# A fused two-model forward pass in fp32: the RMS norms and head norms through one column per token half

## The reference

```python
# first stack, two layers; rmsnorm(x, g) = x * rsqrt(mean(x*x, -1) + eps) * g
x = x + even_mixer(rmsnorm(x, norm_mix[0]), ...)              # gated MLP + forgetting attention
x = x + memory_cross_attention(rmsnorm(x, ...), rmsnorm(mem, ...), ...)
x = x + swiglu(rmsnorm(x, norm_ffn[0]), ...)
x = x + odd_mixer(rmsnorm(x, norm_mix[1]), ...)               # differential attention + short conv
x = x + memory_cross_attention(...)
x = x + moe_swiglu(rmsnorm(x, norm_ffn[1]), ...)              # 8 experts, top 2
x = rmsnorm(x, norm_final)
# second stack, two layers l, modulated by c
h = rms_norm(x, norm1_w[l]) * (1 + sc1) + sh1
x = x + g1 * hybrid_mixer(h, ...)                             # retention + HGRN2
h = rms_norm(x, norm2_w[l]) * (1 + sc2) + sh2
x = x + g2 * conv_ffn(h, ...)
return rms_norm(x, final_norm_w)

def head_norm(o, w):                                          # per head of 128 channels
    return o * rsqrt(mean(o * o, -1) + eps) * w               # then times a silu gate in the second stack
```

## Time and profile before

| | |
|---|---|
| device time, median of 3 runs | 2598.55 us (2595.91 to 2599.55) |
| profiled execution | 2602.0 us, its span 2600.2 us |
| PE busy | 2425.7 us (93%) in 14784 matmul records |
| DVE busy | 1975.0 us (76%) in 2569 |
| ACT busy | 1539.6 us (59%) in 2088 |

### The profile page before, as it was taken

One profiled execution on the slowest core, in us unless ns is written; L12 is line 12 of the kernel. 1 busy time (PEld: TensorE's weight loads), 2 busy tenths in 40 slices (PEclk: granted clock), 3 DMA queues, 4 the chain that ended last, 5 costly groups with the idle time before them and its releaser, 6 DMA issues.

```text
span 2600.2 us, 39070 instructions
## 1 busy us (share of the span) xinstructions
PE 2425.7 (93%) x14784; PEld 2064.8 (79%) x14784; DVE 1975.0 (76%) x2569; ACT 1539.6 (59%) x2088; POOL 4.4 (0%) x8
## 2 busy tenths in 40 slices
PE   7998999989899999999999999997968999976998
PEld 6997998989767676767676767666858998866998
DVE  5755787976488888888888888885766886767664
ACT  4654444445377777777777777775344554543553
POOL 0000000000000000000000000000000000000000
PEclk9999999999899999999999999998988998998999
DMA  8344689544469898989898989891312666421440
GB/s 347 136 156 162 230 305 356 203 162 180 177 259 351 334 352 328 351 328 350 329 350 329 350 328 350 331 386 64 132 65 98 259 236 234 183 76 65 172 170 17
DMA packets 87980, 623.65 MB, mean 240 GB/s; under 512 B 9732, under 2 KB 11304, under 8 KB 12968
## 3 DMA queue, kind: packets, MB, share of 16 engines
q1 hardware_dynamic: 87312, 621.28, 62.9%
q10 hardware_dynamic: 536, 0.53, 0.1%
HBM read 620.72 MB, written 1.05 MB: 239 GB/s over the span
## 4 chain that ended last, share of the span: by engine, by line
PE 89%; DVE 8%; ACT 2%; issue 1%; DMA 0%; ACTq 0%; DVEq 0%; SPq 0%
PE bank L625 13%; PE bank L623 13%; PE bank L624 13%; PE bank L647 11%; PE bank L643 11%; PE bank L644 11%; PE bank L745 2%; PE bank L742 2%; PE bank L744 2%; PE bank L691 2%; PE bank L998 2%; DVE Z L1826 1%; PE bank L935 1%; DVE ring_r L1495 1%; PE bank L946 1%
## 5 line engine op out<-in xcount | busy, mean ns | idle before, releaser
L1495 DVE TENSOR_TENSOR ring_r<-ring,ring_r 128x1024 fp32r<-128x1024 f32 x402 | 490.8, 1224 | 284.5 <-ACT ring_r L1113 284.2
L643 PE MATMUL bank<-XH,ring_r 128*128 128x256 f32 x2208 | 565.7, 292 | 75.4 <-ACT XH L1149 32.1
L1113 ACT ACTIVATE ring_r<-ring 128x1024 fp32r<-128x1024 f32 x402 | 423.5, 1056 | 347.0 <-PE bank L647 176.2
L644 PE MATMUL bank<-XH,ring_r 128*128 128x256 f32 x2208 | 559.9, 289 | 0.0
L643 PEld LDWEIGHTS bank<-XH,ring_r 128*128 128x128 f32 x2208 | 438.7, 199 | 85.5 <-issue 37.0
L1900 DVE TENSOR_TENSOR ring_r<-ring,Z_r 128x1024 fp32r<-128x1024 f32 x336 | 411.1, 1225 | 50.6 <-ACT Z_r L1374 50.6
L644 PEld LDWEIGHTS bank<-XH,ring_r 128*128 128x128 f32 x2208 | 439.1, 199 | 0.1
L1900 DVE TENSOR_TENSOR ring_r<-ring,mhat_r 128x1024 fp32r<-128x1024 f32 x336 | 408.0, 1220 | 36.7 <-ACT mhat_r L1374 35.0
L1374 ACT ACTIVATE mhat_r<-ring 128x1024 fp32r<-128x1024 f32 x336 | 356.3, 1063 | 108.6 <-PE bank L625 106.9
L1374 ACT ACTIVATE Z_r<-ring 128x1024 fp32r<-128x1024 f32 x336 | 356.5, 1062 | 103.8 <-PE bank L625 103.8
L624 PE MATMUL bank<-ring_r,xn_r 128*96 128x512 f32 x896 | 352.2, 393 | 0.0
(11 more groups left out here) (297 smaller groups left out, 3424.9 us busy)
## 6 DMA issues: line engine op xcount, KB each, us to landing
ring<-in_experts SPq DMA_DIRECT2D x336, 1024.0 KB, 6.8
ring<-in_stream SPq DMA_DIRECT2D x246, 1024.0 KB, 7.0
ring<-in_stream SPq DMA_DIRECT2D x6, 512.0 KB, 5.3
xT<-in_xT SPq DMA_DIRECT2D x2, 512.0 KB, 5.3
mhat<-in_memT SPq DMA_DIRECT2D x1, 1024.0 KB, 16.7
swap<-in_early SPq DMA_DIRECT2D x1, 1024.0 KB, 18.6
swap<-in_late SPq DMA_DIRECT2D x1, 1024.0 KB, 9.8
out_T<-xn SPq DMA_DIRECT2D x8, 128.0 KB, 2.0
```

The costliest lines, as they stand in the source:

```text
L643: pe.matmul(dst, hi[:, a], x_hi(kb), start=(n == 0), stop=False)
L644: pe.matmul(dst, lo[:, a], x_hi(kb), start=False, stop=False)
L1113: act.activation(wh(Q), raw(Q), ACT.Copy).then_inc(sems["whi"], 1)
L1495: dve.tensor_tensor(raw(Q, ring_r), raw(Q), wh(Q).bitcast(F32), ALU.subtract).then_inc(sems["wlo"], 1)
```

## The change

The norms' factor is computed once per token on a column instead of on all partitions.

Norms: DVE adds the squares of blocks 1 to 6 (in norms 4, 10 and 12: 1 to 5) onto block 0, each add linked to the one before by a semaphore (`add_squares`). PE then multiplies block 0 and the one (two) left over, as weights, by one column of ones: per block two matmuls, one per half of 128 tokens; the result is 128x2, token on partition. Root and reciprocal run on 128x2 (`rcol`). Two matmuls with the column broadcast as weights and the identity as moving operand spread it over the partitions (`norm_spread`); the apply step reads the factor from PSUM. In norms 1, 2 and 5 the spread comes later in PE's order. ACT's squares of norms 3, 9 and 11 are put between weight quarters.

Head norms: ACT squares each head straight out of PSUM, PE makes eight one-column matmuls, root and reciprocal run on 128x8 (`hcol`), eight matmuls spread them into two banks. Meanwhile DVE multiplies the products, out of PSUM, by gain and gate (`head_scaled`), and by the factor at the end (`head_normed`). In `b{l}` the first spread follows the second group's products on PE.

```diff
-            def norm(i):
-                key = f"nrm{i}"
-                G.wait_free(pe, key)
-                for kb in range(KB):
-                    W(pe, "sq", i, kb + 1)
-                    mm = pe.matmul(bank[G.bank(key)][:, 0:S], ones, sqb(i, kb), start=(kb == 0), stop=(kb == KB - 1))
-                G.filled(mm, key)
+            def norm_sums(i):              # direct(i) is 2 for i in (4, 10, 12), else 1
+                key, first = f"nrm{i}", KB - direct(i)
+                G.wait_free(pe, key)
+                W(pe, "sqa", i)
+                for n, kb in enumerate([0] + list(range(first, KB))):
+                    if n:
+                        W(pe, "sq", i, kb + 1)
+                    for t in range(NT):
+                        mm = pe.matmul(bank[G.bank(key)][:, t:t + 1], sqb(i, kb)[:, t * P:(t + 1) * P], ones[:, 0:1],
+                                       start=(n == 0 and t == 0), stop=(kb == KB - 1), skip_group_check=True)
+                G.filled(mm, key)
+            def norm_spread(i):
+                key = f"spread{i}"
+                G.wait_free(pe, key)
+                W(pe, "rc", i)
+                for t in range(NT):
+                    mm = pe.matmul(bank[G.bank(key)][:, t * P:(t + 1) * P], rcol[:, i % 2, t:t + 1].to_broadcast([P, P]),
+                                   ident, start=True, stop=True)
+                G.filled(mm, key)
+            def head_norm_sums(i, sq):
+                key = f"hn{i}"
+                G.wait_free(pe, key)
+                for h in range(H):
+                    W(pe, "hsq", i, h + 1)
+                    for t in range(NT):
+                        n = 2 * h + t
+                        mm = pe.matmul(bank[G.bank(key)][:, n:n + 1], sq[:, n * P:(n + 1) * P], ones[:, 0:1],
+                                       start=True, stop=True)
+                G.filled(mm, key)
+            def head_norm_spread(i):
+                W(pe, "hrc", i)
+                for g in range(2):
+                    key = f"hb{i}"
+                    G.wait_free(pe, key, g)
+                    for n in range(4):
+                        mm = pe.matmul(bank[G.bank(key, g)][:, n * P:(n + 1) * P],
+                                       hcol[:, 4 * g + n:4 * g + n + 1].to_broadcast([P, P]), ident, start=True, stop=True)
+                    G.filled(mm, key, g)
...
                 linear_pv(f"b{l}.rpv", rv, mhf)
-                head_norm(1 + 2 * l, zs(8))
+                head_norm_sums(1 + 2 * l, zs(8))
...
                 linear_pv(f"b{l}.hpv", hi, zs(0, 2))
-                head_norm(2 + 2 * l, zs(5))
+                head_norm_spread(1 + 2 * l)
+                head_norm_sums(2 + 2 * l, zs(5))
+                head_norm_spread(2 + 2 * l)
...
-            def head_norm(i, pvkey, Y, sq):
+            def head_norm(i, pvkey, sq):
+                for h in range(H):
+                    G.wait_full(act, pvkey, h)
+                    act.activation(sq[:, h * S:(h + 1) * S], bank[G.bank(pvkey, h)][:, 0:S], ACT.Square)\
+                        .then_inc(sems["hsq"], 1)
+                key = f"hn{i}"
+                G.wait_full(act, key)
+                G.drained(act.activation(hcol, bank[G.bank(key)][:, 0:8], ACT.Sqrt, scale=1.0 / P, bias=eps), key)
...
-            def norm(i, src=xT, dst=xn):
+            def add_squares(i, kbs):
+                for kb in kbs:
+                    W(dve, "sq", i, kb + 1)
+                    ins = dve.tensor_tensor(sqb(i, 0), sqb(i, 0), sqb(i, kb), ALU.add)
+                    if kb == KB - direct(i) - 1:
+                        ins.then_inc(sems["sqa"], 1)
+                    else:
+                        dlink(ins)
+            def norm_column(i):
                 G.wait_drained(dve, f"nrm{i}")
-                dlink(dve.reciprocal(rstd[:, :], rms[:, i % 2, :]))
+                dve.reciprocal(rcol[:, i % 2, :], rcol[:, i % 2, :]).then_inc(sems["rc"], 1)
+            def norm_apply(i, src=xT, dst=xn):
+                key = f"spread{i}"
+                G.wait_full(dve, key)
                 g = gcol(i)
                 for kb in range(KB):
-                    dve.scalar_tensor_tensor(out=dst[:, kb, :], in0=src[:, kb, :], scalar=g(kb), in1=rstd[:, :],
-                                             op0=ALU.mult, op1=ALU.mult).then_inc(sems["xn"], 1)
+                    dve.scalar_tensor_tensor(out=dst[:, kb, :], in0=src[:, kb, :], scalar=g(kb),
+                                             in1=bank[G.bank(key)][:, 0:S], op0=ALU.mult, op1=ALU.mult)\
+                        .then_inc(sems["xn"], 1)
+                W(dve, "xn", i, KB)
+                G.drained(dve.memset(tiny[:, 255:256], 0.0), key)
...
             G.drained(dve.tensor_copy(line[:, :], bank[G.bank("line")][0:H, 0:SPAN]), "line")
-            norm(1, mhat, mhat)
+            add_squares(1, range(1, 7))
+            norm_column(1)
...
                     G.drained(ins, key, g)      # residual of ffn{i}, g in 0..3
+                    if g:
+                        add_squares(4 if i == 0 else 8 + 2 * i, ((), (1,), (2, 3), (4, 5))[g])
...
                     residual(f"b{l}.res", o + 16, [m])
                     low()
+                    if m == 4:
+                        add_squares(9 + 2 * l, range(1, 4))
+                    elif m in (5, 6):
+                        add_squares(9 + 2 * l, [m - 1] if m == 5 else [5, 6])
...
-                head_norm(1 + 2 * l, zs(9), zs(8), lambda h: col("ret_w", 4 * l + h), zs(7))
+                head_scaled(1 + 2 * l, f"b{l}.rpv", zs(9), lambda h: col("ret_w", 4 * l + h), zs(7))
+                head_column(1 + 2 * l)
+                for h in range(H):
+                    G.wait_drained(dve, f"b{l}.hg", h)
+                head_scaled(2 + 2 * l, f"b{l}.hpv", zs(10), lambda h: col("hgrn_w", 4 * l + h), zs(3))
+                for h in range(H):
+                    G.wait_drained(dve, f"b{l}.rpv", h)
+                head_normed(1 + 2 * l, zs(9))
+                head_column(2 + 2 * l)
                 rows_low(f"b{l}.out", zs(9), 0)
-                head_norm(2 + 2 * l, zs(10), zs(5), lambda h: col("hgrn_w", 4 * l + h), zs(3))
+                for h in range(H):
+                    G.wait_drained(dve, f"b{l}.hpv", h)
+                head_normed(2 + 2 * l, zs(10))
```

More of the change, by code:

```diff
@@ L393, in build @@
         G.plan("nrm0", 1)
-        for k, n in (("f.q", 4), ("f.f", 1), ("f.k", 4), ("line", 1), ("nrm1", 1), ("f.S", 4), ("f.v", 2), ("f.u", 4),
+        G.plan("spread0", 1)
+        for k, n in (("f.q", 4), ("f.f", 1), ("f.k", 4), ("line", 1), ("nrm1", 1), ("f.S", 4), ("spread1", 1), ("f.v", 2), ("f.u", 4),
                      ("f.vv", 2), ("f.pT", 4), ("f.gm", 4), ("f.pv", 4), ("f.res", 8)):
@@ L398, in plan_mem @@
         def plan_mem(l, i):
-            for k, n in ((f"m{l}.k", 4), (f"nrm{i}", 1), (f"m{l}.k4", 4), (f"m{l}.q", 8), (f"m{l}.S", 4), (f"m{l}.v", 4),
+            for k, n in ((f"m{l}.k", 4), (f"nrm{i}", 1), (f"m{l}.k4", 4), (f"spread{i}", 1),
+                         (f"m{l}.q", 8), (f"m{l}.S", 4), (f"m{l}.v", 4),
                          (f"m{l}.pT", 4), (f"m{l}.pv", 4), (f"m{l}.res", 8)):
@@ L406, in plan_ffn @@
             G.plan(f"nrm{ni}", 1)
+            G.plan(f"spread{ni}", 1)
             for j in range(FB // 2):
@@ L657, in split_ready, with proj_f @@
                         lambda kb: W(pe, "xl", 0, low_base[inst] + order.index(kb) + 1))
-            def proj_f(nm, j, key, x_hi=xh, x_lo=xl, have=(ready, ready), order=range(KB)):
+            def proj_f(nm, j, key, x_hi=xh, x_lo=xl, have=(ready, ready), order=range(KB), between=None):
                 for m in range(4):
+                    if m == 1 and between:
+                        between()
                     i = 4 * j + m
@@ L821, in mem_attention @@
                        (lambda kb: W(pe, "mh", l, kb + 1), lambda kb: W(pe, "ml", l, kb + 1)))
-                norm(ni)
-                proj_f(f"m{l}.k", 1, f"m{l}.k", mh, ml)
+                norm_sums(ni)
+                proj_f(f"m{l}.k", 1, f"m{l}.k", mh, ml, between=lambda: norm_spread(ni))
                 for j in range(2):
@@ L1123, in root @@
                 G.wait_full(act, key)
-                G.drained(act.activation(rms[:, i % 2, :], bank[G.bank(key)][:, 0:S], ACT.Sqrt, scale=1.0 / D, bias=eps),
+                G.drained(act.activation(rcol[:, i % 2, :], bank[G.bank(key)][:, 0:NT], ACT.Sqrt, scale=1.0 / D, bias=eps),
                           key)
@@ L1268, in ffn @@
                 squares(ni, kbs=range(0, 4))
-                prep(3)
-                squares(ni, kbs=range(4, 8))
+                for kb in range(4, 7):
+                    prep()
+                    squares(ni, kbs=[kb])
+                squares(ni, kbs=[7])
                 root(ni)
@@ L1580, in _ @@
             dve.wait_ge(const_in, 32)
+            add_squares(0, range(1, 7))
             norm(0)
@@ L1678, in mem_attention @@
                 vm = zs(4, 2)
-                low(4)
```

(14 more changed lines are left out.)

101 lines of the change are left out of this document (57 added, 44 removed).

## The result

The kernel after takes 2558.19 us (median of 4 runs, 2555.78 to 2559.76) where the kernel before takes 2598.88 (4 runs beside it, 2595.91 to 2599.55): ratio 0.985, 95% interval 0.984 to 0.986, a gain of 40.7 us. The forecast was 2546, its range 2531 to 2563. The direction, the place and the range were right; the gain is 11.6 us less than the 52.3 forecast. The profiled execution took 2559.0 us (span 2557.2), 0.8 above the median, while that of before, at 2602.0, was 3.1 above the 2598.9 measured here. So the two profiles differ by 43.0 us and the medians by 40.7: 2.3 us of the 11.6 are the distance between these executions and their medians, and 9.3 us are terms of the sum (52.3 against 43.0).

The account below looks back on a forecast made before the run. TensorE, with 89% of the chain of waits, plus its holes was taken to bound the kernel. Norms 14.3, late head norms 34 and o layer 4 sum to 52.3 us; 2602.0 less that, less 3.45, gives 2546 us, range 2531 to 2563.

Parts of the forecast that it names:

- What bounds the kernel, and the reciprocals: Whole kernel: TensorE holds 89% of the chain of waits; reciprocals of 6.55 and 1.75 us fall to near 0.2 us.
- Prices: New instructions: one-column matmul 0.22 us at full clock, 0.44 at half; linked add 0.46; apply step 0.48, no more than before.
- C (dear): All 164 new matmuls: broadcast-column weights or one-column matmuls are dear; at 0.82 us each 2644 us; chance 0.04.
- E (free): The 98 one-column sums cost next to nothing, giving back 11 us: 2535 us; chance 0.04.
- Late head norms: Head norms of the two late layers: wait before the output projection goes, 17 us gained a layer, 34 for both.
- Rival A: Late layers pay half clock all through, 8 us a layer: 2562 us; chance 0.14.
- The o layer: Head norm of the o layer: the waiting projection products start at 551.4 instead of 554.42, 4 us gained.
- Norm 1: Norm 1: adds come late, TensorE waits 4.8 us, scores of f.S start at 58.4 instead of 56.35; 2.45 us lost.
- Norms 3 and 4: Norms 3 and 4: linked adds on VectorE delay residuals and sums; 1.2 us lost in norm 3, 1.9 in norm 4.
- Norms 7, 8 and 10: Gains from shorter sums and tails: 2.4 us in norm 7, 0 in norm 8, 2.0 in norm 10.
- The norms as a whole: All thirteen norms: gains and losses of the column form together give 14.3 us gained.
- Rival B: Holes get short enough that the clock holds behind the norms too, 15 us more gained: 2531 us; chance 0.13.

Follow-up runs that it names:

- eighth run: Kernel after with each one-column sum matmul of the two late layers' head norms done twice, 32 records in a row instead of 16: 2568.56 us, ratio 0.990.
- third run: Kernel after with norm 1's six adds moved earlier, three and three behind the first two k-head copies: 2548.03 us, ratio 0.982.
- sixth run: Kernel after with norm 3 summed without adds by sixteen one-column matmuls, norm 4's six adds behind its last residual: 2551.27 us, ratio 0.983.
- seventh kernel: Kernel after with norm 1's adds earlier, norm 3 without adds, norm 4's adds behind its last residual: 2543.55 us, ratio 0.9795; run again 2546.22 us, 0.981.
- fifth run: Kernel after with norm 1 without adds, its sixteen one-column matmuls in two rows behind the first two heads' scores: 2551.48 us, ratio 0.9825.
- second run: Kernel after with the head norms as before, so only the thirteen norms go through columns: 2591.35 us, ratio 0.998.
- fourth run: Kernel after with norm 1 without adds, all eight blocks summed by sixteen one-column matmuls in one row: 2553.91 us, ratio 0.984.
- first run: Kernel before with only the head norms through columns, the thirteen norms as before: 2555.63 us, ratio 0.9845.

## Why the prediction came out as it did

- **What bounds the kernel, and the reciprocals**: right. Reciprocals take 0.17 and 0.20 us.
- **Prices**: right. One-column record at full clock 0.105 us (0.11 said), at half 0.23 (1.84 / 8), four spread records 0.44 where their column is ready. The eight apply steps with an operand in PSUM take 3.22 us, as the old ones did (3.25). Rivals C (dear) and E (free) are out: the eighth run's 32 records took 3.47 us. The Trainium skill's page TensorE: Matmul & The Clock Gate (Back-to-back issue gap) has a floor of 25 ns for a matmul of so few columns, by which, as an estimate, they would take 0.8 us. The same section gives that floor for an isolated gap and says that in a stream of weight load and matmul pairs both set the spacing; the 0.108 us a record here, each with its own weights, agrees with that and not with the floor alone. The prediction set its rows against the floor alone.
- **Late head norms**: right, 17.2 and 17.0 against 17 each, with a hole of 0.59 us where I said 0.7. The 1.5 us missing in the first profile are a clock dip of one execution. Rival A (half clock all through) did not come true, but the eighth run shows that its mechanism is real: rows twice as long bring the half clock.
- **The o layer**: 4.8 and 4.65 against 4. Right.
- **Norm 1, the step that failed most**: "the scores of f.S start at 58.4 ... 2.45 lost". The hole was as said (4.89 us against 4.8). The scores started at 56.47, with norm 0's 2.95 us gained ahead, so 1.0 us later than said. What I left out is that the hole costs the clock: sums at 1.84 instead of 0.87, the scores 10.0 us instead of 6.9. I had priced half clock behind the holes of the other norms, but took this one for a plain wait. The third run removes the hole and gets 8.7 us back.
- **Norms 3 and 4**: the mechanism (linked adds ahead of a residual on DVE) is shown by the sixth run; 0.75 and 0.4 us more than forecast were lost. The sums of norm 4 started 3.8 us later than before's place in the stream, as said.
- **Router and first expert**: the forecast had nothing there. Sixteen L1043 records take 5.41 us where the profile before, the third run and others have 3.91, with PE in the same order of work. The two profiles of the kernel after, the two of the seventh kernel and that of the fifth all lose 2.5 to 2.6 us there; the second, third, fourth and sixth kernel, with the same norm 6, lose nothing. Two stand between: the first, with the old norm 6, loses 1.0 us at the router and nothing in the first expert, and the eighth loses 1.9 us up to 730 and takes 3.91 us in the first expert. So norm 6's new timing is neither needed for the loss at the router nor enough for the rest. It goes with where the clock's turns fall in a given kernel, but which edit moves them is open; no run settled it.
- **Norms 7, 8 and 10**: the table agrees with the forecast (+2.6 against 2.4; 2.0 and 1.0 against 2.0), but the first run had 2.5 and 2.5 there with the old norms. The agreement is no proof of these terms.
- **The norms as a whole**: +14.3 forecast; 3 to 7.5 us alone, about 0 (known to 3.5) on top of the head norms. This is the mis-sized part of the sum, and larger than the 11.6 us by which the gain fell short. The head norms' 38 carry the whole gain. The time came out inside the range because the range was 32 us wide and the head norms gave 1 to 2 us more than forecast, not because the terms of the norms held. With the column norms the mean granted clock is lower in every execution (0.960 to 0.964 against 0.970 to 0.973). That this is what eats the gain of the other norms is likely but not shown; for norm 1 the third run shows it.
- **Rival B** (the clock holds behind the norms): only behind norm 0, where it came back one block earlier, 0.75 us over the forecast. Behind norms 3, 4, 7 and 8 the second run's windows show the opposite, more half clock than with the old norms.

## What to carry to other kernels

A sum over partitions, or a reciprocal of all partitions, can be taken off the path by working on a column, but look where the replacement stands in the other queues: six adds of 0.43 us in front of a waiting TensorE cost 6.6 us, and nothing when they stood three and three in VectorE's queue some 4 to 8 us earlier. Price every new hole with the clock behind it, and treat a long row of one-column matmuls as a hole too: split it with wide matmuls. Before a term of 1 to 3 us is believed from one trace, have a second trace of the old kernel; here there was none, and the one trace was the slowest execution of 38.

## What the runs showed of the hardware that I had not expected

- The granted clock fell to half with TensorE busy 4.00 of 4.00 us: with 32 one-column fp32 records in a row (0.54 in the window of the fourth run, 0.57 in the eighth), while 16 in a row with scores between kept it at 1.00 (fifth run). Eight of eight such rows of 32 brought a fall, and one of 48 rows of 16.
- The clock's turns are not the same in each execution. Norm 1 of the unaltered form lost 5.1, 5.3, 5.4, 5.5 and 6.6 us in five profiles with the same 4.9 us hole, and one spread of 16 records took 2.05 or 3.55 us. The Trainium skill's page TensorE: Matmul & The Clock Gate (Part 1: The HAM clock gate) says of a kernel's start that the same kernel shows different numbers of slow matmuls from run to run; these rows show the like in the middle of one.
- Some of these turns do repeat with the kernel (5.41 us at L1043 in both profiles of the kernel after, 7.14 us at L894 in both of the seventh where the sixth has 8.74), so an edit can move time at a place that it doesn't touch.
